# A two-layer diffusion step in fp32 on one core: conditioning tiles placed between feed-forward blocks, waits for single PSUM sets, unrolled block loops, and another order in the RWKV units

## The reference

```python
def layer(x, cond, l, latent, st):
    sh1, sc1, gt1, sh2, sc2, gt2, sh3, sc3, gt3 = modulation(cond, ada_w[l], ada_b[l])
    h = rms_norm(x, norm_g[l, 0]) * (1 + sc1) + sh1
    x = x + 0.5 * gt1 * swiglu(h, ffn_w1[l, 0], ffn_w2[l, 0])
    h = rms_norm(x, norm_g[l, 1]) * (1 + sc2) + sh2
    p = h @ w_in_even[e]        # layer 0: retention | RWKV-7 ; layer 1: mLSTM | attention
    ...
    x = x + gt2 * mix
    h = rms_norm(x, norm_g[l, 2]) * (1 + sc3) + sh3
    x = x + 0.5 * gt3 * swiglu(h, ffn_w1[l, 1], ffn_w2[l, 1])

def modulation(cond, ada_w, ada_b):
    m = jax.nn.silu(cond) @ ada_w + ada_b            # 1024 -> 9 * 1024, per layer
    return jnp.split(m[:, None, :], N_MOD, axis=-1)
```

## Time and profile before

| | us |
|---|---|
| median of three runs | 3899.51 |
| lowest and highest run | 3883.81 and 3903.02 |
| the profiled execution, by its own timer | 3888.84 |
| its span in the trace | 3887.0 |
| PE busy | 3428.2 |
| DVE busy | 1267.6 |
| ACT busy | 996.1 |
| POOL busy | 336.1 |

### The profile page before, as it was taken

The page is one execution under the profiler, slowest core; times in us unless marked ns, Lnnn a source line. Parts: engine busy times, 40 slices in busy tenths (PEclk is TensorE's granted clock), DMA queues, the critical chain, the costliest instruction groups (busy, mean ns, idle before and its releaser), DMA issues.

```text
span 3887.0 us, 52585 instructions
## 1 busy us (share of the span) xinstructions
PE 3428.2 (88%) x21383; PEld 3045.3 (78%) x21383; DVE 1267.6 (33%) x1862; ACT 996.1 (26%) x1361; POOL 336.1 (9%) x366
## 2 busy tenths in 40 slices
PE   8799998969577877899999979999897689899998
PEld 1399998959466665899998169999897656899998
DVE  0222222245455554322221032222314435322222
ACT  0232122222321122332120033122224435332121
POOL 0000001000444441100000000000101000100001
PEclk9899999969788887999999989999997879999999
DMA  8522121101000000122222822122110100122121
GB/s 312 174 76 77 60 86 55 34 31 50 3 4 1 1 1 22 60 76 76 65 81 78 303 90 82 64 70 81 44 49 12 33 3 27 58 73 76 65 88 42
DMA packets 79087, 260.64 MB, mean 67 GB/s; under 512 B 20112, under 2 KB 20240, under 8 KB 78704
## 3 DMA queue, kind: packets, MB, share of 16 engines
q1 hardware_dynamic: 77568, 250.79, 19.4%
q0 software_dynamic: 1392, 8.07, 0.5%
HBM read 255.02 MB, written 3.81 MB: 67 GB/s over the span
## 4 chain that ended last, share of the span: by engine, by line
PE 82%; DVE 7%; ACT 4%; POOL 3%; issue 3%; DMA 1%; DVEq 0%; SPq 0%; ACTq 0%; POOLq 0%
PE ps L1988 30%; PE ps L1989 30%; PE ps L2009 6%; PE ps L893 1%; PE ps L1817 1%; DVE normed L2266 1%; DVE h_lo L2253 1%; PE ps L884 1%; PE ps L1797 1%; DMA ring<-w_ada 1%; PE ps L1500 1%; POOL h_mem L2357 1%; PE ps L1805 1%; PE ps L873 1%; PE ps L837 1%
## 5 line engine op out<-in xcount | busy, mean ns | idle before, releaser
L315 DVE TENSOR_TENSOR w_lo<-ring,w_hi 128x1024 fp32r<-128x1024 f32 (+1 forms) x305 | 399.0, 1309 | 1867.7 <-ACT w_hi L310 1867.7
L310 ACT ACTIVATE w_hi<-ring 128x1024 fp32r<-128x1024 f32 (+1 forms) x305 | 343.0, 1126 | 1522.0 <-PE ps L1989 1501.8
L1988 PE MATMUL ps<-h_hi,w_hi 128*128 128x320 f32 x1928 | 609.7, 316 | 126.0 <-DVE h_lo L2253 58.5
L1989 PE MATMUL ps<-h_hi,w_hi 128*128 128x320 f32 x1928 | 602.3, 312 | 0.0
L1988 PE MATMUL ps<-h_lo,w_hi 128*128 128x320 f32 x1928 | 601.9, 312 | 0.0
L1989 PE MATMUL ps<-h_lo,w_hi 128*128 128x320 f32 x1928 | 601.8, 312 | 0.0
L1988 PE MATMUL ps<-h_hi,w_lo 128*128 128x320 f32 x1928 | 601.6, 312 | 0.0
L1989 PE MATMUL ps<-h_hi,w_lo 128*128 128x320 f32 x1928 | 601.5, 312 | 0.0
L1988 PEld LDWEIGHTS ps<-h_hi,w_hi 128*128 128x128 f32 x1928 | 367.2, 190 | 145.2 <-issue 80.7
L1989 PEld LDWEIGHTS ps<-h_hi,w_hi 128*128 128x128 f32 x1928 | 368.4, 191 | 0.0
L1988 PEld LDWEIGHTS ps<-h_lo,w_hi 128*128 128x128 f32 x1928 | 367.9, 191 | 0.0
(11 more groups left out here) (348 smaller groups left out, 4527.0 us busy)
## 6 DMA issues: line engine op xcount, KB each, us to landing
ring<-w_ada SPq DMA_DIRECT2D x144, 512.0 KB, 4.5
ring<-w_up0a SPq DMA_DIRECT2D x44, 512.0 KB, 3.4
ring<-w_up0b SPq DMA_DIRECT2D x44, 512.0 KB, 3.3
ring<-w_up1a SPq DMA_DIRECT2D x44, 512.0 KB, 3.3
ring<-w_up1b SPq DMA_DIRECT2D x44, 512.0 KB, 3.3
ring<-w_down0a SPq DMA_DIRECT2D x16, 704.0 KB, 4.0
ring<-w_down0b SPq DMA_DIRECT2D x16, 704.0 KB, 4.0
ring<-w_down1a SPq DMA_DIRECT2D x16, 704.0 KB, 4.1
```

The costliest lines, as they stand in the source:

```text
L310: act.activation(w_hi[:, n % SPLITS, 0:cols], ring[:, r, 0:cols], ACT.Copy).then_inc(high_ready, 1)
L315: dve.tensor_tensor(w_lo[:, n % SPLITS, 0:cols], ring[:, r, 0:cols], w_hi[:, n % SPLITS, 0:cols].bitcast(F32), ALU.subtract).then_inc(spli ...
L1988: pe.matmul(left, weights, acts[:, k, LEFT], start=start, stop=stop)
L1989: mm = pe.matmul(right, weights, acts[:, k, RIGHT], start=start, stop=stop)
```

## The change

**The modulation.** The stage `ada` is gone. A layer's modulation is cut into nine chunks of 1,024 output channels, 8 weight tiles each. Chunks 0 and 1 of layer 0 (shift and scale of the first norm) come first; 7 more go one tile behind each block from `up0a` of layer 0 on, six of layer 1 behind `up1a` of layer 0, the last three behind `up0a` of layer 1: 16 chunks, 128 tiles between blocks. `scond` is widened from 2 to 32 columns with zeros, and a tile is four matmuls of 128 x 32 weights with 256 columns, each into its own 32 partitions of PSUM bank 6 (`modulation_tile`). When a chunk is complete, ACT copies the bank (128 x 256), PE turns it by two transposes into bank 7 (`modulation_turned`), and DVE makes its 16 columns of `mod`. The stream of SP is one list, in which these tiles stand between the blocks' tiles and take slots of the same ring; in these stretches a tile is thus loaded when the one four places ahead is used up, which is two blocks.

**The waits.** `pairs_read`, `free_dve` and `free_act` are gone. A block waits only for the reader of the block that had its PSUM set, now three blocks back; the norms have a set of their own. The first block of a down projection waits for its `g` parts one k at a time.

**The loops.** No hardware loops are left: PE's list grows from 7,228 to 17,084 rows, DVE's from 1,452 to 1,575, ACT's from 936 to 1,064, while SP's goes from 348 to 280 and POOL's from 306 to 308.

**The norms.** A block of `x` is squared in the same step in which it is added, not one later, and this also holds for the first norm of layer 1; in the last block of a stage ahead of a norm DVE adds to `x` before it splits weights.

**The first loads.** POOL loads the identity and the ones (256 of 4,482 columns of the constants, 128 KB) and `x` (2,560 KB); the other constants and `lora` (768 KB) are loaded after the first norm.

**RWKV.** On PE `low_w` goes ahead of step 1 of the core, `low_a` ahead of its `merged`; `matrices` 0 and 1 go behind `widened` 4 and 5, ahead of `merged`; `state` goes behind `merged` 4 and 5; `both_turned` and `natural` 0 go behind `merged` 6. On POOL both late mergings go ahead of `decayed`, which waits for one semaphore step less. On DVE the running sums of the decay are split and start earlier, `masked` 0 and 1 go up, and `first_state` goes down, ahead of `masked` 2. On ACT the two tanh and the exponentials go up.

```diff
-SETS = 4
+SETS = 3
...
+    first_chunks = [(0, m) for m in range(2)]
+    later_chunks = {(0, "up0a"): [(0, m) for m in range(2, N_MOD)], (0, "up1a"): [(1, m) for m in range(6)],
+                    (1, "up0a"): [(1, m) for m in range(6, N_MOD)]}
+    chunk_no = {c: q for q, c in enumerate(first_chunks + [c for cs in later_chunks.values() for c in cs])}
+
+    ada_behind, chunk_behind = {}, {}
+    for stage, chunks in later_chunks.items():
+        for t in range(DB * len(chunks)):
+            ada_behind[block0[stage] + t] = (chunks[t // DB], t % DB)
+        for c, chunk_ in enumerate(chunks):
+            chunk_behind[block0[stage] + DB * c + DB] = chunk_
+
+    loads = [(c, k) for c in first_chunks for k in range(DB)]
+    for b in range(lin):
+        loads.append(b)
+        if b in ada_behind:
+            loads.append(ada_behind[b])
+    place = {t: n for n, t in enumerate(loads)}
...
+            for n, t in enumerate(loads):
+                r = n % RING
+                if n >= RING and isinstance(loads[n - RING], tuple):
+                    sp.wait_ge(ada_used, sum(isinstance(e, tuple) for e in loads[:n - RING + 1]))
+                elif n >= RING:
+                    sp.wait_ge(split_ready, loads[n - RING] + 1)
+                if isinstance(t, tuple):
+                    (layer, m), k = t
+                    sp.dma_start(ring[:, r, 0:D_MODEL], w[layer]["ada"][m * DB + k]).then_inc(land[r], 16)
+                    continue
...
+            readers = {"silu": silu_ready, "prod": prod_ready, "proj": proj_ready, "x": x_ready}
+
+            def modulation_tile(chunk_, k):
+
+                q, n = chunk_no[chunk_], place[chunk_, k]
+                r = n % RING
+                if k == 0 and q:
+                    pe.wait_ge(ada_row_ready, q)
+                pe.wait_ge(land[r], landed[n])
+                for j in range(4):
+                    mm = pe.matmul(bank(6, 0, 2 * P)[32 * j:32 * j + 32], scond[:, k, :],
+                                   ring[:, r, j * 2 * P:(j + 1) * 2 * P], start=(k == 0), stop=(k == DB - 1))
+                mm.then_inc(ada_used, 1)
...
+            def linear(layer, name, n, k_blocks, hi, lo, ready=None):
+
+
+
+                for u in range(n):
+                    b = block0[layer, name] + u
+                    left, right, _ = pair(b % SETS)
+                    s = b % SPLITS
+                    if b >= SETS:
+                        reader, count = read_by[b - SETS]
+                        pe.wait_ge(readers[reader], count)
+                    pe.wait_ge(split_ready, b + 1)
...
+                    if b in chunk_behind:
+                        modulation_turned(chunk_behind[b])
+                    if b in ada_behind:
+                        modulation_tile(*ada_behind[b])
...
-                pairs_read(layer, name)
+                left, right, _ = pair(SETS)
+                if layer < DEPTH:
+                    pe.wait_ge(mod_ready, len(first_chunks) if norms[0] == 0 else chunk_no[layer, 3 * int(name[-1]) + 1] + 1)
...
+                            linear(layer, f"down{j // 2}{half}", DB, HALF_F, g_hi, g_lo,
+                                   ready=(gated_ready, HALF_F * halves))
...
-                    if norm_name is not None and i * 4 + u:
-                        square(norm_name, xn, i * 4 + u - 1)
...
+                    if norm_name is not None:
+                        square(norm_name, xn, u)
...
+                    if not (last_first and u == DB - 1):
+                        part_ahead(dve, b0 + u, low_part)
...
+                    if last_first and u == DB - 1:
+                        part_ahead(dve, b0 + u, low_part)
...
-            pool.dma_start(cst[:, :], consts_in).then_inc(loaded, 16)
-            pool.dma_start(x[:, :, :], x_in).then_inc(loaded, 16)
-            pool.dma_start(lora[:, :, :], lora_in).then_inc(loaded, 16)
+            soon = cat["ones"][1]
+            pool.dma_start(cst[:, 0:soon], consts_in[:, 0:soon]).then_inc(first_loaded, 16)
+            pool.dma_start(x[:, :, :], x_in).then_inc(first_loaded, 16)
...
+                    pool.wait_ge(norm_ready, 1)
+                    pool.dma_start(cst[:, soon:], consts_in[:, soon:]).then_inc(loaded, 16)
+                    pool.dma_start(lora[:, :, :], lora_in).then_inc(loaded, 16)
...
-                        pool.wait_ge(rw_y, 4 * n - 5)
+                        pool.wait_ge(rw_y, 4 * n - 6)
...
                     merging(u, 4)
+                    merging(u, 5)
                 if ahead:
                     decayed(u + 1, 0)
-                if core:
-                    merging(u, 5)
-                if ahead:```

PE around the first norm. Before, its list has the last 16 pieces of the modulation, the transposes, and the sums of the norm (L2029, L2030):

```order
L336 REGISTER_ALU
L336 COMPARE_AND_BRANCH
L2009 MATMUL ps<-ring,scond 2x512 x16
L2018 MATMUL ps<-cst,h_mem 128x2 x72
L2029 MATMUL ps<-h_mem,cst 128x320
L2030 MATMUL ps<-h_mem,cst 128x320
```

More of the change, by code:

```diff
@@ L318, in stepped @@
[L318 to L343, removed]
+        def part_ahead(eng, b, part):
+            n = b + SPLITS
+            if n < lin and not held & {b + 1, n}:
+                part(eng, n)
+        def parts_first(eng, b, part):
+            if b in held:
+                for n in range(b, b + SPLITS):
+                    part(eng, n)
@@ new lines, in high_part, with low_part @@
+        def high_part(act, b):
+            r, cols = place[b] % RING, cols_of[b]
+            act.wait_ge(land[r], landed[place[b]])
+            if b >= SPLITS:
+                act.wait_ge(tiles_done, b + 1 - SPLITS)
+            act.activation(w_hi[:, b % SPLITS, 0:cols], ring[:, r, 0:cols], ACT.Copy).then_inc(high_ready, 1)
+        def low_part(dve, b):
+            r, cols = place[b] % RING, cols_of[b]
+            dve.wait_ge(high_ready, b + 1)
+            dve.tensor_tensor(w_lo[:, b % SPLITS, 0:cols], ring[:, r, 0:cols],
+                              w_hi[:, b % SPLITS, 0:cols].bitcast(F32), ALU.subtract).then_inc(split_ready, 1)
@@ L984, in tensor_rwkv @@
                 core, ahead, behind = 0 <= u < RW_N, u + 1 < RW_N, u >= 1
+                if ahead and u >= 0:
+                    low_w(u + 1)
                 if core:
@@ L1012, in tensor_rwkv @@
                     widened(u, 4)
-                if behind:
-                    state(u - 1, 0)
+                if ahead:
+                    matrices(u + 1, 0)
                 if core:
@@ L1375, in vector_rwkv @@
                     other_half(u + 1, 1)
+                if ahead and u >= 1:
+                    first_state(u + 1)
+                if ahead:
                     masked(u + 1, 2)
@@ new lines, in _ @@
+            for n, t in enumerate(loads):
+                r = n % RING
[6 more added lines that the diff above has]
+                    sp.dma_start(ring[:, r, 0:D_MODEL], w[layer]["ada"][m * DB + k]).then_inc(land[r], 16)
+                    continue
+                layer, name, u = stage_of[t]
+                if u == 0 and name in ("rwkv", "att", "out"):
+                    sp.wait_ge(mix_ready, 4 * (1 + (name == "out")) + 8 * layer)
+                    if name != "out":
+                        sp.wait_ge(saved, 16 * (2 if layer == 0 else 8))
+                dst, parts = ring[:, r, 0:cols_of[t]], parts_of(layer, name, u)
+                if len(parts) == 1:
+                    sp.dma_start(dst, parts[0]).then_inc(land[r], 16)
+                    continue
+                for half, part in enumerate(parts):
+                    sp.dma_start(dst.rearrange("p (k t c) -> p k t c", t=2, c=HS)[:, :, half, :], part)\
+                      .then_inc(land[r], 16)
@@ L2315, in _ @@
+            for chunk_ in first_chunks:
+                modulation(chunk_)
             for layer in range(DEPTH):
-                modulation(layer)
                 for j in range(3):
```

435 lines of the change are left out of this document (178 added, 257 removed).

## The result

The changed kernel takes 3576.87 us (median of four runs, 3575.50 to 3578.74), where the kernel before takes 3901.27 beside it. The ratio is 0.918, with a 95% interval of 0.915 to 0.921. The profiled execution took 3575.50, 313.3 less than the 3888.84 of before.

A forecast was written before the change was run, and what follows sets the result against it. PE bounds the kernel, busy 88% of the span and 82% of the last chain. Terms -117 - 146.5 + 96 - 84 - 21 - 10 = -282.5 take profiled 3888.84 to 3606; the median's 10.7 makes 3617 us, range 3560 to 3710.

The forecast's parts named there:

- Start: Up to layer 0's first block: 16 tiles instead of 72 ahead, bound by transfers, block at about 57; -117 us.
- Layer 1's modulation: Gap between layer 0's last down matmul and layer 1's first up block: 157.7 us shrinks to a norm's 11.2; -146.5 us.
- norms: PE's gap at each norm: earlier sums and add cut 15.5 us to 11.2; -21 us with the last norm.
- Tiles: 128 modulation tiles between blocks: four column strips overlapping, 0.72 us a tile; +96 us with transposes.
- the rivals with fewer strips at once: Modulation tiles: strips two at a time, +55, 3672 us, chance 0.12; one at a time, +154, 3771, chance 0.05.
- Seams: Between up and down stages: PE's waits (41.4 and 15.7) and the slow clock behind them (17.6 and 9.7) go; -84 us.
- RWKV: RWKV units: list reordering saves 6.0 us of waits against 5.0 added, one us a unit over ten units; -10 us.
- The bounds of -50 to +50: RWKV stage: a unit may go 5 us either way, -50 to +50 us over all.
- RWKV better: RWKV units 4 us cheaper each than before, kernel at 3577 us; chance 0.07.
- Median: Whole kernel: the median stands 10.7 us above the profiled run, added to 3606 to give 3617.
- Instruction fetch: Dense stages without loops: about 88 more code pieces; one us each gives 3705 (mild, chance 0.03), 3.5 gives 3925 (0.02).
- ring: Mixed stretches of blocks and modulation tiles: PE waits for weights, one us for each of 128 tiles, 3745; chance 0.05.

The follow-up runs named there:

- x_tail: Changed kernel with `masked` 2 one step up on DVE and, on ACT, `natural` 0 first and `spread_state` last: 3534.37 us (0.908 of before).
- f_rwkv: Changed kernel with 12 unused identity matmuls in each RWKV unit, behind `natural` 0 and ahead of `matrices` 3: 3558.77 us (0.914 of before).

## Why the prediction was right, and where its sizes were off

- **Start.** Right to 4 us: bound by transfers. The last tile and the first square came 2 us later than the 33 and 34, POOL's sums took 1.6 longer.
- **Layer 1's modulation, norms.** Right to 2 us. 10.55 in every one, where 11.2 was forecast: the 7 us behind the sums stayed, as read, and the part ahead of them shrank to 3.56 instead of some 4.1.
- **Tiles.** 0.77 instead of 0.72, 102 instead of 96. The row of two strips gave the overlap of four and the cost of the change of shape (0.1 in, 0.1 at the next matmul); the rivals with fewer strips at once are ruled out by the timeline and by doubling them.
- **Seams.** -84.0, the number forecast, and near it in both halves: 59 us of waits gone (57 forecast), and 25 us of stages that no longer start at half clock (27). Undoing the waits gave 70 of it back.
- **RWKV.** The step that failed. The sum of that step, 6.0 us of waits saved against 5.0 added in a unit, came out near for waits: 13 us less idle over ten units, where it said 10. That is partly luck, as two of its terms were off: `first_state` took 0.49 us in its new place, not 1.39, and the wait at L884 was put down to `merging` 5, with which it does not return. Above all, the step counted waits alone. At the seams the same prediction had counted the half clock behind a stall; in RWKV, where the rows showed a clock of 0.83 over 565 us, it did not ask what the clock would do. Of the 47 us some 38 are the clock. The bounds of -50 to +50 held it, and the rival "RWKV better" (3577, chance 0.07) is the case that came, though for another reason than waits. That the time meets its 3577 to within 1 us is luck: RWKV gave 37 us more than forecast and the median's distance 9, while tiles and start cost 10 more.
- **Median.** The 10.7 us that were added for the distance of the profiled run from the median were wrong: they belong to the old RWKV order, whose runs scatter by 15 to 20 us with the clock, and went with it.
- **Instruction fetch and ring.** 84 pieces more, where 88 were worked out, and no pause in a dense stage. PE waits 16 times for tiles of the modulation, 18.0 us in all, and these are the 16 at the start; between blocks it waits for none.

## What to carry to other kernels

Where PE waits a few microseconds in a repeated unit, cost the stretch at half clock that follows as well as the wait: here it was over three quarters of the RWKV stage's gain, and a wait that was only moved cost more than it had. How long the stretch lasts can't be told from the wait (91 and 153 us behind the same ones), so an order is compared by its clock, measured. Follow such a wait through the engines until nothing regular is left (two edits, on DVE and ACT, gave 42 us together, the first alone lost 31), and where it can't be removed, matmuls on constants in the gap are worth a try (18 and 41 us here). A side product with few rows was cheap in column strips between the blocks of a dense stage: four strips cost the time of one.

## What the runs showed that was not expected

- In the RWKV units a wait of 3.6 to 4.1 us was followed by the lower of the two clock levels (0.50 in the rows); in x_tail, where that place has 0.9 us, the units stayed at 1.00, and in f_rwkv, with 0.9 behind the filler, but for two stretches of 3.4 us that began in the middle of a unit, behind waits of 0.7 to 1.5 us close together. How long it stayed down after the same wait varied between units of one execution. These two windows are of the kernel before, one spell and the one ahead of it, with the waits that they stand behind:

```profile
1255.30:1272.30 17.00, 15.10 (x64) 13.08 (x65) 6.23 (x9) 2.42 (x4) 6.14 (x5) 0.50 0.00 0
1211.00:1214.00 3.00, 3.00 (x12) 1.92 (x12) 0.92 (x1) 0.00 (x0) 3.00 (x3) 0.50 0.00 0
...
1256.51 2.08 PE L837 MATMUL ps<-w_mem 64*128 64x256 f32 x8 [4.06 <-DVE w_mem L1240]
1210.96 2.08 PE L837 MATMUL ps<-w_mem 64*128 64x256 f32 x8 [4.06 <-DVE w_mem L1240]
```

- Both stand behind the same wait of 4.06 us in two units that follow each other; one lasted 17 us, the other 3. Between 1105 and 1422 us of that trace the lengths behind this wait come back every third unit, 17, 17 and 3 us; in the changed kernel they are 10, 3 and 3. What decides them stays open: the work behind the wait is the same.
- A microsecond at half clock cost the stage 0.38 to 0.42 us, less than the half that a PE without waits would lose. PE is busy in 77% of the stage after (397.93 of 518.07 us), and half of that is 0.38: an estimate that fits, not an experiment.
